# Causal mask of a differential-attention kernel: a TensorE matmul into the score block in place of a VectorE add

## The chip, the cores and the metric

One core of one Trainium2 chip runs the whole step as one program. The metric is the device time of that program in microseconds (us). TensorE (PE) multiplies, VectorE (DVE), ScalarE (ACT) and GpSimd (POOL) do the rest, SyncE (SP) issues most transfers. Each engine works through its own instructions in order and waits on semaphores for the others. A matmul has a weight operand, loaded into TensorE first (LDWEIGHTS, shown as PEld), and a moving operand that is streamed through it; products are summed in PSUM.

## The reference, cut to what matters

One inference step of a two-layer trunk with D = 1024 and a prompt of 1024 tokens: a matrix-memory layer, then a differential-attention layer, plus eight decode sequences. The change touches only the attention of the prompt. For each of 8 heads there are two sets of queries and keys (c = 0 and 1, 64 columns each), a causal softmax over each, and a difference of the two weights:

```python
def diff_mix(q, k_parts, v_parts, masks, lam):
    scores = []
    for kp, mk in zip(k_parts, masks):
        s = jnp.einsum('bqhcd,bkhcd->bhcqk', q, kp).astype(F32) * ATTN_SCALE
        if mk is not None:
            s = jnp.where(mk, s, -jnp.inf)        # mask = qpos >= kpos
        scores.append(s)
    p = jax.nn.softmax(jnp.concatenate(scores, axis=-1), axis=-1)
    w = p[:, :, 0] - lam * p[:, :, 1]
...
        o = jnp.einsum('bhqk,bkhe->bqhe', w[..., start:start + s_len].astype(vp.dtype), vp)
```

All is held to float32; the kernel splits operands into a high part and a remainder (names ending in H and L), so a product becomes three matmuls: high by high, high by low, low by high.

## The kernel before, in words

The phases follow each other: norm, gates, matrix memory for the prompt, the same for the samples, its output projection, then `attention_phase` (the one touched), decode, and the last projection.

`attention_phase` goes head by head. Head 0's `sweep1` comes first; then a hardware loop (`Fori` in `heads`) runs `sweep2(h)` and `sweep1(h+1)` for h = 0 to 6; head 7's `sweep2` and a `tail` follow as straight code. The order on each engine is simply the order of the code; semaphores tie the engines together.

- `sweep1` projects queries and keys (`project(0, t)`: 24 matmuls of 256 columns for each of nine token blocks), rotates them on VectorE and transposes them into `QTH`, `QTL`, `KTH`, `KTL`. There the two components lie on partitions 0 to 63 (c = 0) and 64 to 127 (c = 1).
- `sweep2` takes the eight query blocks t = 0 to 7 in turn. On TensorE the order for t is `scores(h, t)` (L1836), `turn_weights(h, t-1)` (transposes, L1857), `project_values(t+1)` (24 matmuls, L1831), `turn_output(h, t-2)` (L1877), `weigh(h, t-1)` (weights by values, L1869).
- `scores` computes for each c the block's scores against all keys up to the diagonal: three matmuls with 64 weight rows (L1846) for each chunk of up to 512 columns. The width is rounded up to a multiple of 256: 256 columns at t = 0 and 1, 512 at 2 and 3, 768 (a chunk of 512 and one of 256) at 4 and 5, 1024 at 6 and 7. The two components write different PSUM tensors, `S[0]` and `S[1]`. The last matmul of each component raises `sc`.
- VectorE, on `sc`, adds the triangular mask `cst[:, C_MB:...]` (0 or -1e30) to the diagonal 128 columns of `S[c]` in PSUM (L1792), takes the row maximum (L1794) and scales it (L1795, raises `mxs`). `links.link` makes the next instruction wait until the linked one has ended.
- ScalarE exponentiates on `mxs` (L1634) and raises `ex`. VectorE then cuts the next head's weights (L1696), forms the difference of the two softmaxes (L1809 to L1812, raises `ww`), and `turn_weights` on TensorE waits for `ww`.
- `scores(h, t)` itself waits for `ex` of block t-1, since it overwrites `S[c]`; `project_values(t+1)` waits for `vz`, the evacuation of the values by ScalarE (L1584 to L1586).

Of the kernel before, what the change touches and what calls it, by code (L numbers as in the profile page):

```python
# [17 lines left out]
ALU = mybir.AluOpType  # L18
ACT = mybir.ActivationFunctionType
F32 = mybir.dt.float32  # L20
F32R = mybir.dt.float32r
# [3 lines left out]
P = 128  # L25
# [21 lines left out]
C_MB = C_MA + P  # L47
# [59 lines left out]
def trunk_step(  # L107
# [8 lines left out]
    def sb(name, shape, dt=F32):  # L116
        return ctx.enter_context(nc.sbuf_tensor(name, shape, dt))
# [3 lines left out]
    def sem(name):  # L121

        held.append(nc.alloc_semaphore(name=name))
        return held[-1]
# [3 lines left out]
    def phase_tensor(name, shape, dt=F32):  # L128

        return scratch[-1].enter_context(nc.sbuf_tensor(name, shape, dt))  # L130
# [13 lines left out]
    def two(name):  # L144
        return [sem(f"{name}{k}") for k in range(2)]
# [12 lines left out]
    with ctx:  # L158

        cst = sb("cst", [P, C_N])  # L160
        ident = cst[:, C_ID:C_ID + P]
# [1316 lines left out]
        def attention_phase():  # L1478
# [14 lines left out]
            KR = RAW[:, 4 * KT * P:5 * KT * P].rearrange("p (t c) -> p t c", t=NT)  # L1493
            QTR = phase_tensor("QTR", [P, 2, SEQ], F32R)
            QTH, QTL = QTR[:, 0, :], QTR[:, 1, :]
            KTH = WH[:, 4 * KT * P:5 * KT * P]
            KTL = WL[:, 4 * KT * P:5 * KT * P]
            N = 2 * P
# [4 lines left out]
            pj, rope, kr, kth, vz, sc, mxs, ex, ww, av, ot, otf, sq, rr, sg, gz, yy, smd = (  # L1503
                sem(f"c_{s}") for s in ("pj", "rope", "kr", "kth", "vz", "sc", "mx", "ex", "w", "av",
                                        "ot", "otf", "sq", "rr", "sg", "gz", "y", "sm"))
            tr, trf, wt, wte = two("c_tr"), two("c_trf"), two("c_wt"), two("c_wte")
            dch, pch = sem("c_dve"), sem("c_pool")
            B_V, B_O = BK[0], BK[1]
            S = [PD[c][:, :, :].rearrange("p a n -> p (a n)") for c in range(2)]
# [3 lines left out]
            def heads(eng, sweep1, sweep2, tail, links=None, per=0):  # L1513

                sweep1(0, None)
                with eng.Fori(0, H - 1) as h:
                    if links:
                        links.enter(h, per)
                    sweep2(h, False)
                    sweep1(h + 1, h)  # L1520
                if links:
                    links.leave(H - 1)
                sweep2(H - 1, True)
                tail(H - 1)

            with nc.Block() as block:
# [40 lines left out]
                def _(act):  # L1567
                    def cut(r, k):
                        for j, (_, _, g) in enumerate(PARTS[r]):
                            cols = slice(j * P, (j + 1) * P)  # L1570
                            act.activation(reg(WH, r)[:, k, cols], reg(RAW, r)[:, k, cols], ACT.Copy,
                                           scale=g[:, k:k + 1]).then_inc(hi[r], 1)

                    act.wait_ge(lamS, 1)
                    act.activation(le, mx, ACT.Exp).then_inc(lamE, 1)

# [26 lines left out]
                    def sweep1(h, before):  # L1603
                        act.wait_ge(c_w[1], 32 * (h + 1))
                        act.wait_ge(pj, 2 * NB * h)
                        for t in range(NB):
# [6 lines left out]
                            if t >= 1:  # L1613
                                c = t - 1
                                act.wait_ge(tr[c % 2], 4 * h + c // 2 + 1)
                                act.activation(QTH[:, c * P:(c + 1) * P], BK[2 + c % 2][:, 0:P], ACT.Copy)
                                act.activation(KTH[:, c * P:(c + 1) * P], BK[2 + c % 2][:, P:2 * P], ACT.Copy)\
                                   .then_inc(kth, 1)
# [68 lines left out]
                def _(dve):  # L1687
                    v = nc.vector
                    links = Chain(dve, dch)
# [58 lines left out]
                    def weights(h, c):  # L1748

                        m = c - 3  # L1750
                        dve.wait_ge(wt[1], 4 * h + m)
                        v.tensor_copy(WT[:, 4:4 + m, :], BK[3][:, 0:m * P].rearrange("p (a c) -> p a c", a=m))\
                         .then_inc(wte[1], 1)

                    def sweep1(h, before):
                        for t in range(NB):
# [11 lines left out]
                            if t >= 1:  # L1768
# [3 lines left out]
                                v.tensor_tensor(QTL[:, tt], BK[2 + c % 2][:, 0:P], QTH[:, tt].bitcast(F32), ALU.subtract)  # L1772
                                v.tensor_tensor(KTL[:, tt], BK[2 + c % 2][:, P:2 * P], KTH[:, tt].bitcast(F32),
                                                ALU.subtract).then_inc(trf[c % 2], 1)
# [7 lines left out]
                    def sweep2(h, last):  # L1782
                        for t in range(NB):
                            n = (t + 1) * P
                            if t < NT:
                                for c in range(2):
                                    if c == 1 and t > 4:
                                        weights(h, t - 1)
                                    if c == 1 and t >= 2:
                                        output(h, t - 2)  # L1790
                                    dve.wait_ge(sc, 2 * (NT * h + t) + c + 1)
                                    links.link(v.tensor_tensor(S[c][:, n - P:n], S[c][:, n - P:n],  # L1792
                                                               cst[:, C_MB:C_MB + P], ALU.add))
                                    links.link(v.tensor_reduce(mx[:, c:c + 1], S[c][:, 0:n], AX, ALU.max, negate=True))  # L1794
                                    v.tensor_scalar(nm[:, c:c + 1], mx[:, c:c + 1], ATTN_SCALE, None, ALU.mult)\  # L1795
                                     .then_inc(mxs, 1)
                            if t == NT:
                                output(h, t - 2)
                            if t >= 3:
                                o_transposed(h, t - 3)  # L1800
                            if t >= 1:
                                sigmoid(h, t - 1)
                            if t < NT:
                                if not last:
                                    cut(0, t, h)

                                b = t % 2
                                dve.wait_ge(ex, 2 * (NT * h + t) + 2)
                                links.link(v.reciprocal(cf, sm[:, 1:2]))  # L1809
                                links.link(v.scalar_tensor_tensor(cf, sm[:, 0:1], nl, cf, ALU.mult, ALU.mult))  # L1810
                                v.reciprocal(rc[:, b:b + 1], sm[:, 0:1])
                                v.scalar_tensor_tensor(PR[:, 0, 0:n], PR[:, 1, 0:n], cf, PR[:, 0, 0:n],  # L1812
                                                       ALU.mult, ALU.add).then_inc(ww, 1)
                                dve.wait_ge(ww, NT * h + t + 1)

                    def tail(h):
# [1 line left out]
                        output(h, NT - 1)  # L1818
                        o_transposed(h, NT - 2)
                        o_transposed(h, NT - 1)  # L1820
                    heads(dve, sweep1, sweep2, tail, links, 9 + 8 * 2 * 2 + 16)

                @block.tensor
                def _(pe):
# [11 lines left out]
                    def scores(h, t):  # L1836
                        width = (t // 2 + 1) * 2 * P
                        for c in range(2):

                            pe.wait_ge(ex, 2 * NT * h + max(2 * t - 1 + c, 0))  # L1840
                            rows = slice(DK * c, DK * c + DK)
                            for at in range(0, width, 512):
                                kk = slice(at, min(at + 512, width))
                                i = 0
                                for q, k in ((QTH, KTH), (QTH, KTL), (QTL, KTH)):
                                    x = nc.tensor.matmul(S[c][:, kk], q[rows, t * P:(t + 1) * P], k[rows, kk],  # L1846
                                                         start=(i == 0), stop=(i == 2))
                                    i += 1
                            x.then_inc(sc, 1)

                    def turn_weights(h, c):
                        pe.wait_ge(ww, NT * h + c + 1)
# [51 lines left out]
                    def sweep2(h, last):  # L1904
                        def project_values(t):

                            pe.wait_ge(vz, NT * h + t)
                            pe.wait_ge(smd, h)
                            project(1, t, B_V)

                        pe.wait_ge(hi[1], 2 * KT * (h + 1))
                        pe.wait_ge(lo[1], 2 * KT * (h + 1))
                        project_values(0)
                        for b in range(2):
                            pe.wait_ge(trf[b], 4 * (h + 1))
                        pe.wait_ge(rope, NB * (h + 1))
                        scores(h, 0)
                        project_values(1)
                        for t in range(1, NT):
                            scores(h, t)  # L1920
                            turn_weights(h, t - 1)
                            project_values(t + 1)
                            if t >= 2:
                                turn_output(h, t - 2)
                            weigh(h, t - 1)
# [400 lines left out]
        run(out_phase, "oa", w_out_a, True)  # L2326
        fresh_semaphores()
        run(attention_phase)
        run(decode_phase)
        run(out_phase, "ob", w_out_b, False)  # L2330
# [31 lines left out]
```

## Time and profile before

| | |
|---|---|
| median of 3 runs | 2084.65 us (2083.03 to 2088.9) |
| span of the profiled execution, first to last instruction | 2078.4 us |
| PE busy over the span | 1826.7 us, 88% |
| DVE busy | 1153.2 us, 55% |
| ACT busy | 806.3 us, 39% |
| mean granted TensorE clock | 0.928 |

The page gives the profiled execution's span and no separate run time for it; the median lies 6.25 us above the span, which is what lies around it. The attention of the prompt runs from about 950 us to 1643 us of the span; its `sweep2` work begins at 986 us. Busy time of a matmul group is the union of its records, and records of pipelined matmuls overlap; for what a matmul costs in a stream, the distance between two starts is to be read, not the duration.

### The profile page before, as it was taken

How to read it: one execution, taken by the hardware profiler on the slowest of the kernel's cores; microseconds unless marked ns; L12 is line 12 of the kernel's file. 1: busy time of each engine (PE TensorE's matmuls, PEld its weight loads, DVE VectorE, ACT ScalarE, POOL GpSimd, SP SyncE). 2: the span in 40 equal slices, each digit the busy share in tenths (PEclk: the TensorE clock that was granted, in tenths of full speed). 3: DMA queues.
4: the chain of work that ended last, by engine and by line, in shares of the span. 5: the costliest groups of instructions: out<-in, count | busy, mean ns of one | idle time of the engine just before them, and what ended most of it. 6: DMA issues, size and time to landing. Idle time of an engine off the chain costs nothing. (4 is left out here: it accounts for less than half of the span.)

```text
span 2078.4 us, 40295 instructions
## 1 busy us (share of the span) xinstructions
PE 1826.7 (88%) x13011; PEld 1669.8 (80%) x13011; DVE 1153.2 (55%) x3279; ACT 806.3 (39%) x2208; POOL 379.9 (18%) x823
## 2 busy tenths in 40 slices
PE   5499999999999675998999999999999688888598
PEld 4399999999999564998889898898989666665398
DVE  4443544443443354246767667676677566666533
ACT  5333333333333223033534435344353356666401
POOL 1021221221221121011312213122131100101101
PEclk8699999999999776999999999999999888989699
DMA  4213113113211134222011120111200267777522
GB/s 118 64 32 65 31 33 65 34 30 65 34 30 15 39 88 131 78 103 87 26 50 32 31 63 12 51 32 31 63 12 11 82 228 257 257 243 241 157 73 84
DMA packets 157012, 165.21 MB, mean 79 GB/s; under 512 B 12314, under 2 KB 134266, under 8 KB 156914
## 3 DMA queue, kind: packets, MB, share of 16 engines
q1 hardware_dynamic: 152610, 159.85, 26.2%
q0 software_dynamic: 1184, 4.23, 0.8%
q8 instruction: 39, 0.64, 0.1%
q14 instruction: 59, 0.48, 0.1%
q10 hardware_dynamic: 3120, 0.01, 0.1%
HBM read 138.69 MB, written 25.37 MB: 79 GB/s over the span
## 5 line engine op out<-in xcount | busy, mean ns | idle before, releaser
L809 PE MATMUL PS<-WH,XH 128*128 128x384 f32 (+3 forms) x1152 | 369.4, 321 | 1.8 <-DVE WORK L731 1.8
L809 PE MATMUL PS<-WL,XH 128*128 128x384 f32 (+3 forms) x1152 | 356.9, 310 | 0.0
L809 PE MATMUL PS<-WH,XL 128*128 128x384 f32 (+3 forms) x1152 | 356.6, 310 | 0.0
L809 PEld LDWEIGHTS PS<-WH,XH 128*128 128x128 f32 (+1 forms) x1152 | 208.1, 181 | 6.6 <-DVE WORK L731 2.2
L809 PEld LDWEIGHTS PS<-WL,XH 128*128 128x128 f32 (+1 forms) x1152 | 208.2, 181 | 4.1
L809 PEld LDWEIGHTS PS<-WH,XL 128*128 128x128 f32 (+1 forms) x1152 | 207.8, 180 | 4.6
L1432 PE MATMUL PS<-WH,XH 128*128 128x256 f32 (+1 forms) x576 | 166.2, 289 | 34.4 <-DVE WL L1305 28.6
L1831 PE MATMUL PS<-WH,XH 128*128 128x256 f32 (+1 forms) x576 | 173.6, 301 | 2.3 <-ACT WORK L1586 2.1
L1831 PE MATMUL PD<-WH,XH 128*128 128x256 f32 (+1 forms) x576 | 169.4, 294 | 2.9 <-PEq L142 2.9
L1831 PE MATMUL PS<-WL,XH 128*128 128x256 f32 (+1 forms) x576 | 167.4, 291 | 0.0
L1831 PE MATMUL PS<-WH,XL 128*128 128x256 f32 (+1 forms) x576 | 167.0, 290 | 0.0
L1432 PE MATMUL PS<-WL,XH 128*128 128x256 f32 (+1 forms) x576 | 165.3, 287 | 0.0
L1432 PE MATMUL PS<-WH,XL 128*128 128x256 f32 (+1 forms) x576 | 164.0, 285 | 0.0
L1831 PE MATMUL PD<-WL,XH 128*128 128x256 f32 (+1 forms) x576 | 163.9, 284 | 0.0
L1831 PE MATMUL PD<-WH,XL 128*128 128x256 f32 (+1 forms) x576 | 163.6, 284 | 0.0
L1432 PEld LDWEIGHTS PS<-WH,XH 128*128 128x128 f32 (+1 forms) x576 | 106.3, 185 | 37.9 <-issue 33.0
L1634 ACT ACTIVATE WORK<-PD,WORK 128x256 f32<-128x256 f32 (+7 forms) x128 | 95.0, 742 | 82.0 <-DVE WORK L1795 81.3
L2258 PE MATMUL PS<-cst,RAW 128*128 128x128 f32 x512 | 87.3, 322 | 40.3 <-DVE XL L2165 35.9
L2258 PEld LDWEIGHTS PS<-cst,RAW 128*128 128x128 f32 x512 | 68.4, 164 | 58.5 <-DVE XL L2165 42.8
L1831 PEld LDWEIGHTS PS<-WH,XH 128*128 128x128 f32 (+1 forms) x576 | 108.8, 189 | 4.8 <-ACT WORK L1586 3.9
L1831 PEld LDWEIGHTS PS<-WH,XL 128*128 128x128 f32 (+1 forms) x576 | 108.9, 189 | 0.7
L1831 PEld LDWEIGHTS PS<-WL,XH 128*128 128x128 f32 (+1 forms) x576 | 108.8, 189 | 0.6
(335 smaller groups left out, 4411.3 us busy)
## 6 DMA issues: line engine op xcount, KB each, us to landing
RAW<-in_cache_k SPq DMA_DIRECT2D x64, 512.0 KB, 4.5
WORK<-in_cache_v SPq DMA_DIRECT2D x64, 512.0 KB, 4.4
RAW<-in_w_in_a SPq DMA_DIRECT2D x40, 512.0 KB, 6.3
RAW<-in_w_in_b SPq DMA_DIRECT2D x16, 512.0 KB, 6.3
RAW<-in_w_kv SPq DMA_DIRECT2D x16, 512.0 KB, 5.2
out<-WORK SPq DMA_DIRECT2D x16, 512.0 KB, 2.9
WORK<-in_x_prompt SPq DMA_DIRECT2D x8, 512.0 KB, 4.9
WORK<-d_G SPq DMA_DIRECT2D x8, 512.0 KB
```

The costliest lines, as they stand in the source:

```text
L809: last = nc.tensor.matmul(bank[0:rows, 0:n], x[:, k, tt], reg(w)[:, k, :], start=(i == 0), stop=(i == 3 * KT - 1))
L1432: last = nc.tensor.matmul(BK[u % 2][0:rows, 0:N], x[:, k, tt], reg(w, r)[:, k, :], start=(n == 0), stop=(n == 3 * KT - 1))
L1634: act.activation(PR[:, c, 0:(t + 1) * P], S[c][:, 0:(t + 1) * P], ACT.Exp, scale=ATTN_SCALE, bias=nm[:, c:c + 1], accum_out=sm[:, c:c + 1] ...
L1831: last = nc.tensor.matmul(bank[0:rows, 0:N], x[:, k, tt], reg(w, r)[:, k, :], start=(i == 0), stop=(i == 3 * KT - 1))
L2258: x = nc.tensor.transpose(BK[j][:, h * P:(h + 1) * P], KB[:, p % 4, (4 * j + h) * P:(4 * j + h + 1) * P], ident)
```

## The change

ScalarE copies the identity and the mask once, at the start of the phase, into a new tensor `MR` of TensorE's input type. After the score matmuls of a component, TensorE multiplies the identity (128 weight rows by 128 columns) with the mask (128 columns) and lets the product accumulate onto the diagonal columns of `S[c]`; that matmul now raises `sc`. VectorE's add is gone. The number of linked instructions that VectorE counts per loop turn falls by 16.

```diff
+            MR = phase_tensor("MR", [P, 2, P], F32R)
...
+            mr = sem("c_mr")
...
+                    act.activation(MR[:, 0, :], ident, ACT.Copy)
+                    act.activation(MR[:, 1, :], cst[:, C_MB:C_MB + P], ACT.Copy).then_inc(mr, 1)
                     act.wait_ge(lamS, 1)
...
                                     dve.wait_ge(sc, 2 * (NT * h + t) + c + 1)
-                                    links.link(v.tensor_tensor(S[c][:, n - P:n], S[c][:, n - P:n],
-                                                               cst[:, C_MB:C_MB + P], ALU.add))
                                     links.link(v.tensor_reduce(mx[:, c:c + 1], S[c][:, 0:n], AX, ALU.max, negate=True))
...
-                    heads(dve, sweep1, sweep2, tail, links, 9 + 8 * 2 * 2 + 16)
+                    heads(dve, sweep1, sweep2, tail, links, 9 + 8 * 2 + 16)
...
-                                    x = nc.tensor.matmul(S[c][:, kk], q[rows, t * P:(t + 1) * P], k[rows, kk],
-                                                         start=(i == 0), stop=(i == 2))
+                                    nc.tensor.matmul(S[c][:, kk], q[rows, t * P:(t + 1) * P], k[rows, kk],
+                                                     start=(i == 0), stop=(i == 2))
                                     i += 1
-                            x.then_inc(sc, 1)
+                            nc.tensor.matmul(S[c][:, t * P:(t + 1) * P], MR[:, 0, :], MR[:, 1, :], start=False, stop=True,
+                                             skip_group_check=True).then_inc(sc, 1)
...
+                        pe.wait_ge(mr, 1)
                         scores(h, 0)
```

On TensorE, at `scores(h, 2)` inside the loop, the program before has the three matmuls of c = 0, those of c = 1 and then the transposes (the rows name output and operands; L1840 sets a register for a wait):

```order
L1846 MATMUL PD<-WH,QTR 128x512
L1846 MATMUL PD<-WL,QTR 128x512
L1846 MATMUL PD<-WH,QTR 128x512
L1840 REGISTER_ALU
L1846 MATMUL PD<-WH,QTR 128x512
L1846 MATMUL PD<-WL,QTR 128x512
L1846 MATMUL PD<-WH,QTR 128x512
L1857 MATMUL PS<-cst,WORK 128x128 x2
```

The same place in the changed program, where lines below the edits count a few higher:

```order
L1848 MATMUL PD<-WH,QTR 128x512
L1848 MATMUL PD<-WL,QTR 128x512
L1848 MATMUL PD<-WH,QTR 128x512
L1851 MATMUL PD<-MR 128x128
L1842 REGISTER_ALU
L1848 MATMUL PD<-WH,QTR 128x512
L1848 MATMUL PD<-WL,QTR 128x512
L1848 MATMUL PD<-WH,QTR 128x512
L1851 MATMUL PD<-MR 128x128
L1860 MATMUL PS<-cst,WORK 128x128 x2
```

One matmul of 128 weight rows now stands between the two components, and one between the second component and the transposes.

On VectorE, at the start of a query block in the loop before:

```order
L1792 TENSOR_TENSOR PD<-PD,cst 128x128
L97 REGISTER_ALU
L1794 TENSOR_REDUCE WORK<-PD 128x1
L97 REGISTER_ALU
L1795 TENSOR_SCALAR WORK<-WORK 128x1
```

and in the changed program:

```order
L1796 TENSOR_REDUCE WORK<-PD 128x1
L97 REGISTER_ALU
L1797 TENSOR_SCALAR WORK<-WORK 128x1
```

The add and the wait for its end are gone from the head of the chain; nothing else on VectorE has moved.

## Rows read from the trace of the kernel before

**Rows 1.** The page: its head line.

```profile
span 2078.4 us, 40295 instructions
```

**Rows 2.** Busy time by engine in one window: time, busy time (instructions), clock, DMA.

```profile
985.00:1640.00 655.00, 625.00 (x4842) 578.67 (x4841) 463.09 (x1513) 292.31 (x983) 154.83 (x373) 0.98 0.13 35
```

**Rows 3.** DVE groups, 985 to 1640 us: count, busy us, mean ns, idle before.

```profile
L1792 DVE TENSOR_TENSOR PD<-PD,cst 128x128 f32<-128x128 f32 x128 | 37.9, 296 | 61.6 <-issue 33.4 <-PE PD L1846 24.4
```

**Rows 4.** PE waits, 985 to 1640 us: total us, times, longest.

```profile
PE PD L1846 <- ACT WORK L1634: 11.5, 6, 2.2
...
PE PS L1877 <- DVE YX L1738: 2.7, 9, 0.7
```

**Rows 5.** PE in order of time, scores(3, 2): start, us, instruction.

```profile
1255.21 0.50 PE L1846 MATMUL PD<-WH,QTR 64*128 64x512 f32 x2
1255.55 0.40 PE L1846 MATMUL PD<-WL,QTR 64*128 64x512 f32 x2
1255.78 0.40 PE L1846 MATMUL PD<-WH,QTR 64*128 64x512 f32 x2
1256.11 0.44 PE L1857 MATMUL PS<-cst,WORK 128*128 128x128 f32 x2
```

**Rows 6.** PE in order of time, a stream of projection matmuls before transposes.

```profile
1297.49 0.28 PE L1831 MATMUL PD<-WH,XL 128*128 128x256 f32 x1
1297.61 1.03 PE L1857 MATMUL PS<-cst,WORK 128*128 128x128 f32 x8
1298.40 0.36 PE L1831 MATMUL PD<-WH,XH 128*128 128x256 f32 x1
```

**Rows 7.** PE in order of time, weights by values (eight products, sixteen records).

```profile
1301.44 1.95 PE L1869 MATMUL PS<-WORK 128*128 128x128 f32 x16
1303.23 0.27 PE L1901 MATMUL PS<-cst,WORK 128*128 128x128 f32 x1
```

**Rows 8.** PE in order of time, scores(3, 3).

```profile
1259.94 0.51 PE L1846 MATMUL PD<-WH,QTR 64*128 64x512 f32 x2
...
1261.32 0.55 PE L1857 MATMUL PS<-cst,WORK 128*128 128x128 f32 x3 [0.41 <-DVE WORK L1812]
```

**Rows 9.** PE in order of time, scores(3, 4).

```profile
1265.46 0.49 PE L1846 MATMUL PD<-WH,QTR 64*128 64x512 f32 x1
...
1267.08 0.28 PE L1846 MATMUL PD<-WH,QTR 64*128 64x256 f32 x1
1267.29 0.66 PE L1857 MATMUL PS<-cst,WORK 128*128 128x128 f32 x4
```

**Rows 10.** PE in order of time, scores(3, 7).

```profile
1286.49 0.50 PE L1846 MATMUL PD<-WH,QTR 64*128 64x512 f32 x1
...
1288.66 0.98 PE L1857 MATMUL PS<-cst,WORK 128*128 128x128 f32 x7
```

**Rows 11.** All engines in order of time, head 3 from block 0 to 1.

```profile
1246.20 0.30 DVE L1792 TENSOR_TENSOR PD<-PD,cst 128x128 f32<-128x128 f32 x1 [5.22 <-issue]
1246.53 0.29 DVE L1794 TENSOR_REDUCE WORK<-PD 128x1 f32<-128x128 f32 x1
...
1247.55 0.39 PE L1846 MATMUL PD<-WH,QTR 64*128 64x256 f32 x1 [1.58 <-ACT WORK L1634]
...
1250.26 0.33 PE L1857 MATMUL PS<-cst,WORK 128*128 128x128 f32 x1 [1.33 <-DVE WORK L1812]
```

**Rows 12.** PE in order of time, head 7, blocks 0 and 1.

```profile
1587.97 0.39 PE L1846 MATMUL PD<-WH,QTR 64*128 64x256 f32 x2
1588.19 0.29 PE L1846 MATMUL PD<-WL,QTR 64*128 64x256 f32 x2
1588.31 0.28 PE L1846 MATMUL PD<-WH,QTR 64*128 64x256 f32 x2
1588.74 0.39 PE L1831 MATMUL PS<-WH,XH 128*128 128x256 f32 x1
```

**Rows 13.** PE in order of time, the tail of head 7.

```profile
1635.09 1.09 PE L1857 MATMUL PS<-cst,WORK 128*128 128x128 f32 x8 [0.75 <-DVE WORK L1812]
```

## The prediction

> **What bounds the kernel now.** I began with the head line of the page for the span [rows 1], then took the busy time of the stretch from 985 to 1640 us, in which the score blocks lie. TensorE is busy for 625 of 655 us there and VectorE for 463, at a mean granted clock of 0.98, so nearly all of it at the 2.4 GHz level [rows 2]. TensorE is the bound of the stretch: what the change puts on it counts, and what it takes from VectorE counts only where TensorE stood waiting for VectorE. Next I took VectorE's group of mask adds, to see what is removed: 128 adds, 37.9 us busy, and VectorE idle 61.6 us before them [rows 3]. An engine that sits idle in front of the instruction is not short of time for it. Then TensorE's waits: those before the scores sum to 11.5 us in six times, and those before the output transposes to 2.7 us in nine [rows 4]. Last, TensorE in order of time through single score blocks, since the cost lies in how these matmuls follow each other.
>
> That view shows what decides the case. For block 2 the six score matmuls of 512 columns start in pairs: two at 1255.21, two at 1255.55, two at 1255.78, and the transposes follow at 1256.11 [rows 5]. By the program, three of them are of c = 0 and the other three, behind these, of c = 1. The two components have 64 weight rows each, on different halves of the array, and run side by side: six matmuls take 0.90 us, where the spacing of one component alone is 0.34, 0.23 and 0.33. From the same rows, a component of one 512 chunk takes 0.90 us whether or not the other runs beside it; so the second component is free. The new mask matmul has 128 weight rows, stands between the two components in program order, and needs both halves.
>
> The rule of the Trainium skill that speaks to this is in "TensorEngine Tiling (Array Packing)", section Tiling Modes: tiles work independently of each other, and a change of tiling mode drains the engine. The pairs agree with its first half [rows 5], and so do the 0.34 us after the first matmul of a mode against 0.23 later with its second.
>
> **The change part by part.** (1) *The overlap goes.* After the change the order is c = 0, mask, c = 1, mask, transposes. The first mask must wait for all of c = 0, and c = 1 waits behind it. Call B the time of one component, from its first start to the start of a 128-row matmul behind it. For blocks 2 and 3, B = 0.90 [rows 5]. For blocks 4 and 5 three matmuls of 256 columns are added at 0.12 us, the spacing of such matmuls in a stream [rows 6]: 1.26. For 6 and 7 three more of 512 at 0.23 [rows 5]: 1.59. For blocks 0 and 1 (256 columns) 0.22 + 0.12 [rows 12] plus the 0.21 from a last 256-column matmul to the transposes [rows 9]: 0.55. Return to 64 rows after the first mask costs 0.09 more than a start behind a matmul of the same mode; I take it from the exit, 0.33 against 0.23 [rows 5] or 0.21 against 0.12 [rows 9, 6].
>
> (2) *The mask matmul itself*, m. No matmul of this operand type with only 128 moving columns is in the trace. From below: a transpose with the same shape, one record each, 0.79 us for eight or 0.10 us, say 0.11 [rows 6]. From above: a float32 product of that shape, two records each, 1.79 us for eight or 0.22 us [rows 7]. Nothing excludes either. The code itself rounds score widths up to 256 columns, which pays only if narrower matmuls of this type gain nothing; and a 256-column one takes 0.12. I take 0.22, the row that is a matmul and not a transpose.
>
> So a score block costs 2B + 2m + 0.09 = 2B + 0.53 where nothing hides it:
> - block 2: 1.80 + 0.53 = 2.33, before 0.90 [rows 5]: +1.43
> - block 3: 2.33, before 1.38, of which 0.41 was a wait for VectorE that the longer block now covers [rows 8]: +0.95
> - blocks 4 and 5: 2.52 + 0.53 = 3.05, before 1.83 [rows 9]: +1.22 each
> - blocks 6 and 7: 3.18 + 0.53 = 3.71, before 2.17 [rows 10]: +1.54 each
>
> Together 7.90 us a head. Blocks 0 and 1 of heads 1 to 6 cost nothing: at each turn of the loop VectorE starts some 5 us late (5.22 idle on nothing that the profile shows, at 1246.20), and TensorE then stands 1.58 us before the scores of block 1 and 1.33 us before the transposes of block 0 [rows 11]. Six such stalls are what stands in the waits before the scores [rows 4]. Block 0 grows by about 0.9 us, block 1 by at most 1.1, and both fall into these waits.
>
> (3) *What VectorE gives back.* An add and its link take 0.33 us, from 1246.20 to 1246.53 [rows 11]. Where TensorE waits on this chain the gain is two adds, 0.65 us, once a loop head, at the transposes of block 0. Elsewhere TensorE doesn't wait for the chain, and it is worth nothing. The short waits before the output transposes, 2.7 us in nine [rows 4], are covered by the longer block 7: 0.23 a head, which leaves part of the tail's.
>
> A loop head then costs 7.90 - 0.65 - 0.23 = 7.02 us; six of them 42.1 us. Heads 0 and 7 have no late start. Head 7's block 0 took 0.77 with its wait [rows 12] and now 2 x 0.55 + 0.53 = 1.63: +0.86; block 1 about +1.1 (0.55 before, by B, without the wait); block 3 had no wait there, +1.43; so 0.86 + 1.1 + 1.43 + 1.43 + 5.52 = 10.3. In its tail TensorE waited 0.75 us for VectorE's last weights [rows 13]; VectorE now ends 0.2 to 0.65 us earlier, and with the 0.23 about 1.0 comes back: 9.3. Head 0 has the two small waits of blocks 2 and 3 instead; I take 9.3 for it too.
>
> Sum: 42.1 + 18.6 = 60.7 us. With m = 0.11, 104 exposed masks (12 in each loop head, 16 in each of the other two) cost 11.4 us less: 49. If no wait covers anything, the six loop heads pay 0.65 + 0.23 + 0.43 and up to 2 us more each, some 80 in all; I see no reason for that but keep it as the far end.
>
> (4) *Edits at nothing.* ScalarE's two copies into `MR` stand at the start of the phase, before it waits for the transfers of the lambda vectors, and TensorE's wait on them ends long before the first scores. If that cover were gone they cost well under 1 us, once. The new operand of the mask matmul needs no transfer. The semaphore now comes 0.3 to 0.5 us later for c = 0 and later still for c = 1; behind it on VectorE are the maximum, the output scaling and the next head's weight cuts, but without the adds VectorE reaches the weights at about the same time, and TensorE asks for them 1 to 1.5 us later.
>
> The span goes from 2078.4 to 2139 us [rows 1]; the median stands 6.25 us above the span, so 2145 us.
>
> **The rivals.** *The second component passes the mask* (the halves stay side by side because TensorE orders the work by array half and the mask costs its own place only). Then a block costs 2m more: 12 masks a head at 0.11 to 0.22 is 1.3 to 2.6 us, less about 1.3 a loop head for the waits; in all +3 to +15 us, 2088 to 2100. For it: TensorE already starts c = 1 ahead of two earlier matmuls of c = 0 [rows 5]. Against it: the mask reads and fills both halves, so c = 1's weights would overwrite it. The skill's page "TensorE: Matmul & The Clock Gate", Part 3, has matmuls start strictly in program order; by that rule there would be little overlap to lose and this rival's time would come out. The pairs that start together do not agree with it [rows 5].
>
> *VectorE's chain is what TensorE waits for* and the masks hide in the remaining waits. That ends faster: 0.65 and 0.23 for six loop heads, 0.41 at block 3 in seven heads and the tail's 0.75 give about -9 us, 2076. It decides if the masks run within the waits of blocks 0, 1 and 3. For it: those waits exist [rows 8, 11]. Against it: blocks 2 and 4 to 7 have none [rows 5, 9, 10].
>
> *Every change of mode costs more than the rows show*, because two full changes now stand in each block with weights of both kinds. At 0.2 us more for each of the 104 exposed masks, twice the 0.1 that a change of mode shows [rows 5], this is +21 us on the forecast, 2166.
>
> **How the numbers follow.** Forecast 0.80, with its own range 2130 to 2160 (m from 0.11 to 0.22 and more of the waits used up or left); second component passes 0.12, a third of it within 0.3%; VectorE's chain 0.04, three quarters of it beyond 0.3%; dearer changes of mode 0.04. A change of 0.3%, 6 us, is about what a measurement of this kernel can tell from none. Faster 0.03, same 0.05, slower 0.92. The range 2115 to 2165 holds most of the forecast and the dear case and stops short of the cheap ones.
>
> **What would show it.** Right: in the changed profile the scores of c = 1 start after the first mask of the block; block 2 takes 2.2 to 2.4 us from first score to transposes, block 6 about 3.6; the waits before the transposes of block 3 are gone; VectorE's idle time before the maximum grows. Wrong: score matmuls still in pairs; a stretch from 985 us that is not longer by 45 to 65 us; a mask matmul that follows the last score at a distance beyond 0.4 us; or a gain before the transposes of block 0 in place of a loss.

## The result, and the profile after

The changed kernel takes 2121.8 us (median of 4 runs, 2115.55 to 2128.17) against 2084.09 us for the kernel before (4 runs): a ratio of 1.0172, 95% interval 1.0152 to 1.0192. It is slower by some 37 us (38 by the medians, 36 by the ratio). The forecast was 2145 us, slower by 61; the direction and the mechanism came out, the size was too large by 23. The measured time lies within the stated range of 2115 to 2165, but below the 2130 to 2160 that the forecast gave for itself.

The head line of its page, then its busy time by engine in the window of the score blocks (time, busy us and instructions of PE, PEld, DVE, ACT and POOL, granted clock, DMA):

```profile
span 2119.2 us, 40320 instructions
```

```profile
993.00:1683.00 690.00, 676.23 (x4960) 612.99 (x4959) 426.30 (x1384) 284.59 (x984) 142.23 (x376) 1.00 0.12 33
```

TensorE is now busy for 676 of 690 us where it was for 625 of 655 [rows 2]; VectorE has lost 37 us of work, and the stretch has become longer all the same. Two details matter below: TensorE's idle time fell from 30 to 14 us, and the mean granted clock rose from 0.98 to 1.00.

VectorE's maximum, now the first of its chain, by count, busy us, mean ns and idle before it with its releasers:

```profile
L1796 DVE TENSOR_REDUCE WORK<-PD 128x1 f32<-128x256 f32 (+7 forms) x128 | 96.7, 755 | 98.6 <-PE PD L1851 63.1 <-issue 33.6
```

VectorE waits 63.1 us for the mask matmul (L1851) where it waited 24.4 us for the scores, then in front of its add [rows 3]. The work taken from it turned into waiting.

TensorE in order of time through block 2 of head 3 (start, duration, instruction), the place of [rows 5]:

```profile
1273.05 0.50 PE L1848 MATMUL PD<-WH,QTR 64*128 64x512 f32 x1
1273.39 0.39 PE L1848 MATMUL PD<-WL,QTR 64*128 64x512 f32 x1
1273.62 0.39 PE L1848 MATMUL PD<-WH,QTR 64*128 64x512 f32 x1
1273.94 0.33 PE L1851 MATMUL PD<-MR 128*128 128x128 f32 x1
1274.20 0.49 PE L1848 MATMUL PD<-WH,QTR 64*128 64x512 f32 x1
1274.53 0.39 PE L1848 MATMUL PD<-WL,QTR 64*128 64x512 f32 x1
1274.77 0.39 PE L1848 MATMUL PD<-WH,QTR 64*128 64x512 f32 x1
1275.09 0.33 PE L1851 MATMUL PD<-MR 128*128 128x128 f32 x1
1275.25 0.40 PE L1860 MATMUL PS<-cst,WORK 128*128 128x128 f32 x2
```

No pair starts together any more. Component 0 takes 0.89 us to its mask, component 1 starts 0.26 us behind that mask and takes 0.89 us to the second one: 2.20 us to the transposes instead of 0.90. Block 7 of the same head, the place of [rows 10], goes from 2.17 to 3.62 us:

```profile
1309.00 0.50 PE L1848 MATMUL PD<-WH,QTR 64*128 64x512 f32 x1
...
1312.62 0.51 PE L1860 MATMUL PS<-cst,WORK 128*128 128x128 f32 x3
```

The start of that head, the place of [rows 11]:

```profile
1266.41 0.29 DVE L1796 TENSOR_REDUCE WORK<-PD 128x1 f32<-128x128 f32 x1 [5.45 <-issue]
...
1267.44 0.39 PE L1848 MATMUL PD<-WH,QTR 64*128 64x256 f32 x1 [0.96 <-ACT WORK L1638]
...
1269.61 0.33 PE L1860 MATMUL PS<-cst,WORK 128*128 128x128 f32 x1 [0.49 <-DVE WORK L1814]
```

VectorE still starts late. From its first instruction to the transposes it is 3.20 us, before 4.06: the shorter chain shows here. TensorE's own waits in the whole stretch, engine and line, what for, total us, times, longest:

```profile
PE PD L1848 <- ACT WORK L1638: 6.8, 6, 1.5
PE PS L1860 <- DVE WORK L1814: 3.7, 7, 0.7
PE PS L1880 <- DVE YX L1742: 0.7, 1, 0.7
```

They answer to 11.5 us before the scores and 2.7 us before the output transposes [rows 4], and to this line of the same view before, for the waits ahead of the transposes of the weights:

```profile
PE PS L1857 <- DVE WORK L1812: 11.1, 14, 1.3
```

From the first scores of head 0 to the last output transpose it is 690.8 us (992.94 to 1683.73) against 656.1 (986.22 to 1642.29): +34.7 us. The spans differ by 40.8 us: 6.7 us more stand before the first scores, and 0.6 us less behind the last output transpose. The change has only ScalarE's two copies into `MR` there, which end at 956.1 us, some 37 us ahead of the first scores; over the profiles of this study the first scores start between 983.0 and 993.3 us, at 991.3 in one without those copies (filled waits, below). The 6.25 us that were said to lie around the span are not all of that kind: in the runs whose time and span are both known the two are 1.7 us apart (2120.93 and 2119.2 us for the profiled run here). By the same distance the execution profiled before would have taken 2080.1 us (an estimate), 4.5 us below its median, so the difference of the two spans is larger than that of the times.

### The profile page after: what moved, and what is told of

It is laid out like the page before. It is cut to its first block and busy times, and to the rows that moved or that the text cites. A ratio compares the mean times of both kernels' runs of the same rounds, so it can differ in the third digit from the quotient of the medians.

```text
span 2119.2 us, 40320 instructions
## 1 busy us (share of the span) xinstructions
PE 1883.3 (89%) x13139; PEld 1709.0 (81%) x13139; DVE 1115.8 (53%) x3151; ACT 799.0 (38%) x2210; POOL 366.2 (17%) x823
## 5 line engine op out<-in xcount | busy, mean ns | idle before, releaser
L809 PEld LDWEIGHTS PS<-WH,XH 128*128 128x128 f32 (+1 forms) x1152 | 208.0, 181 | 7.3 <-DVE WORK L731 2.9
L809 PEld LDWEIGHTS PS<-WL,XH 128*128 128x128 f32 (+1 forms) x1152 | 208.2, 181 | 4.1
L809 PEld LDWEIGHTS PS<-WH,XL 128*128 128x128 f32 (+1 forms) x1152 | 207.5, 180 | 4.6
L1432 PE MATMUL PS<-WH,XH 128*128 128x256 f32 (+1 forms) x576 | 166.3, 289 | 34.9 <-DVE WL L1305 28.8
L1833 PE MATMUL PS<-WH,XH 128*128 128x256 f32 (+1 forms) x576 | 168.7, 293 | 0.0
L1796 DVE TENSOR_REDUCE WORK<-PD 128x1 f32<-128x256 f32 (+7 forms) x128 | 96.7, 755 | 98.6 <-PE PD L1851 63.1
L1848 PE MATMUL PD<-WH,QTR 64*128 64x512 f32 (+1 forms) x384 | 136.4, 389 | 6.8 <-ACT WORK L1638 6.8
L1432 PEld LDWEIGHTS PS<-WH,XH 128*128 128x128 f32 (+1 forms) x576 | 106.4, 185 | 38.3 <-issue 33.1
L1833 PEld LDWEIGHTS PD<-WH,XH 128*128 128x128 f32 (+1 forms) x576 | 105.3, 183 | 3.4 <-issue 3.0
```

What stands on the lines that cost most here:

```text
L809: last = nc.tensor.matmul(bank[0:rows, 0:n], x[:, k, tt], reg(w)[:, k, :], start=(i == 0), stop=(i == 3 * KT - 1))
L1432: last = nc.tensor.matmul(BK[u % 2][0:rows, 0:N], x[:, k, tt], reg(w, r)[:, k, :], start=(n == 0), stop=(n == 3 * KT - 1))
L1833: last = nc.tensor.matmul(bank[0:rows, 0:N], x[:, k, tt], reg(w, r)[:, k, :], start=(i == 0), stop=(i == 3 * KT - 1))
```

## The experiments

Three questions were open: whether the cost is the cut overlap or the mask matmul itself; what VectorE's relief was worth; and why the loss was 35 us where the sum had said 61.

**Masks behind both components.** Both mask matmuls of a block stand behind the scores of both components; nothing else differs from the changed kernel.

```diff
+                        for c in range(2):
                             nc.tensor.matmul(S[c][:, t * P:(t + 1) * P], MR[:, 0, :], MR[:, 1, :], start=False, stop=True,
                                              skip_group_check=True).then_inc(sc, 1)
```

> The two mask matmuls stand behind the scores of both components (c = 0, c = 1, mask 0, mask 1). Theory (the loss is the overlap of the two 64-row components, cut by a 128-row matmul between them): score matmuls start in pairs again; block 2 takes 0.90 + 0.22 = 1.12 us from first score to transposes instead of 2.20, block 7 about 2.4 instead of 3.62; the whole is 2074 to 2090 us, the loss of 37 us all but gone. Rival (the mask matmul itself is what costs, 0.27 us or more for each of 104): pairs may come back, but the time stays at 2105 to 2118.

2079.14 us, ratio to before 0.9978 (0.9965 to 0.9991). TensorE in order of time, block 2 of head 3:

```profile
1256.13 0.50 PE L1848 MATMUL PD<-WH,QTR 64*128 64x512 f32 x2
1256.46 0.40 PE L1848 MATMUL PD<-WL,QTR 64*128 64x512 f32 x2
1256.69 0.40 PE L1848 MATMUL PD<-WH,QTR 64*128 64x512 f32 x2
1257.03 0.44 PE L1852 MATMUL PD<-MR 128*128 128x128 f32 x2
1257.30 0.41 PE L1861 MATMUL PS<-cst,WORK 128*128 128x128 f32 x2
```

The pairs are back, the two masks cost 0.27 us, and the whole loss of 37 us has gone with one change of order. The same 128 mask matmuls run in both kernels, so the overlap is what the change paid with. The new order also saves changes between 64 and 128 weight rows, but these are the smaller part: of the 1.03 us between 2.20 and 1.17 us for block 2, 0.89 is the time of component 1, and 0.15 is what the two masks take more between the components than side by side (0.26 + 0.16 us from each mask to the next start, against 0.27 for both).

**Each mask twice.** The changed kernel with a second, equal mask matmul behind each; the masked scores get -2e30.

> The changed kernel with each mask matmul issued twice (the masked scores get -2e30). It measures one mask in a stream: 104 exposed. At 0.11 us each (the pace of a transpose) 11 us above the changed kernel, 2133; at the 0.22 that the prediction took, 23 us, 2145.

2131.32 us, ratio 1.0232 (1.0212 to 1.0252), about 0.6% or 12 us above the changed kernel's ratio. TensorE, block 2 of head 3, from the first mask on:

```profile
1280.25 0.33 PE L1851 MATMUL PD<-MR 128*128 128x128 f32 x1
1280.42 0.28 PE L1853 MATMUL PD<-MR 128*128 128x128 f32 x1
1280.62 0.50 PE L1848 MATMUL PD<-WH,QTR 64*128 64x512 f32 x1
```

The start of component 1 moves from 0.26 us behind the first mask to 0.37: a mask in a stream is 0.11 us, the lower bound of the prediction, not the 0.22 that it took. The starts decide this rather than the whole time, since in this profile all six loop heads also lose time to the clock (below), which only two do in the changed kernel's.

**No mask at all.** The kernel before without VectorE's add and with nothing in its place (the attention is not causal within the diagonal block).

```diff
-                                    links.link(v.tensor_tensor(S[c][:, n - P:n], S[c][:, n - P:n],
-                                                               cst[:, C_MB:C_MB + P], ALU.add))
```

> The kernel before with VectorE's add left out and nothing in its place, so the attention of the prompt is not causal within the diagonal block. It shows what the removal alone gives. Theory (VectorE is off the path but for the start of each loop head, and the waits there also lower TensorE's clock for 3.4 to 6.8 us each): 9 us from the waits and some of the 12 us that the six half-clock stretches cost, 2064 to 2075. Rival without the clock: the waits alone, 2073 to 2077. Rival that VectorE's chain is the bound: 38 us or more, below 2046.

2060.12 us, ratio 0.9899 (0.9879 to 0.9919), below the 2064 to 2075 expected. The relief of VectorE is worth 21 us, more than the waits alone (9) that the prediction's rival had counted and less than the adds' 38 us. The half-clock stretches, places behind the start of heads 1 to 6 where the granted clock is at the 1.2 GHz level (shown under the filled waits), had no part in it; all six were still there. Reading the starts of each block from the trace in order of time, a loop head (one of heads 1 to 6, from its first scores to those of the next head) loses 2.8 us: 0.9 at its start, 0.5 before the transposes of block 2, and 1.4 us in the late blocks 5 to 7, where the prediction had counted 0.23.

**The kept add.** The changed kernel with VectorE's add as well, to see what covers those late waits.

> The changed kernel with VectorE's add kept as well (the mask is applied twice, the masked scores get -2e30). It asks what covers the short waits of blocks 5 to 7 in the changed kernel. If it is the longer score blocks, the stretches from the transposes of blocks 4, 5 and 6 stay at 4.74, 5.08 and 8.37 us, and only the start of a loop head gets 0.6 us longer, six times: 2124 to 2130 with the clock as it falls. If it is the shorter VectorE chain, they go back to 5.2, 5.5 and 8.9 and the whole to 2133 to 2138.

2138.41 us, ratio 1.0242 (1.0226 to 1.0258). Neither expectation holds alone. From the transposes of block 4, 5 and 6 to the next block (the last to the transposes of block 7), means of heads 1 to 6: before 5.22, 5.54 and 8.94 us; changed 4.74, 5.08 and 8.37; with the add kept 4.74, 5.33 and 8.70. The longer score blocks cover 0.93 of the 1.51 us, and with them in place the shorter VectorE chain gives the other 0.58. These are not two separate shares: without a mask, with short score blocks, the shorter chain alone took 1.40 us off the same stretches (4.79, 5.10 and 8.41), and with the masks behind both components it took 0.64 (4.81, 5.43 and 8.82).

**The early copy** (e5 in the later expectations). The kernel before, with VectorE's copy of the transposed output ahead of the maximum of c = 1.

```diff
                                     if c == 1 and t >= 2:
                                         output(h, t - 2)
+                                    if c == 1 and t >= 3:
+                                        o_transposed(h, t - 3)
...
-                            if t >= 3:
+                            if t == NT:
                                 o_transposed(h, t - 3)
```

> The kernel before with one move in VectorE's order: the copy of the transposed output (o_transposed of block t-3) stands ahead of the maximum of c = 1 instead of behind it. Theory (in blocks 5 to 7 TensorE waits shortly for that copy because VectorE's chain, mask adds included, holds it up; the removed adds repaid this too, about 1.4 us a head): the stretches from the transposes of block 4, 5 and 6 to the next block fall from 5.22, 5.54 and 8.94 to about 4.8, 5.1 and 8.4 us, the whole by 8 to 12 us, to 2071 to 2076. Rival (those stretches are TensorE's own work): no change, 2083.

2084.77 us, ratio 1.0010 (0.9998 to 1.0022): no gain. The first two stretches fell as expected, to 4.78 and 5.11, so TensorE had waited there for this copy. But the third rose, from 8.94 to 9.68 us, and the copy now stands ahead of the maximum. TensorE, block 7 of head 3, in order of time:

```profile
1291.45 0.50 PE L1848 MATMUL PD<-WH,QTR 64*128 64x512 f32 x1
...
1294.11 0.66 PE L1859 MATMUL PS<-cst,WORK 128*128 128x128 f32 x4 [0.42 <-DVE WORK L1814]
```

Block 7 takes 2.66 us where it took 2.17 [rows 10], and a loop head 87.55 us where it took 86.79. TensorE now waits 0.42 us for VectorE before the transposes there. The wait only moved.

**Filled waits** (e4). The kernel before, with 10 matmuls of 256 columns before the scores of block 1 and 8 before the transposes of block 0, into columns of `S[0]` that nothing reads.

```diff
+                    def warm(n):
+                        for _ in range(n):
+                            nc.tensor.matmul(S[0][:, 512:512 + N], XH[:, 0, 0:P], reg(WH, 1)[:, 0, :], start=True, stop=True)
...
+                            if t == 1:
+                                warm(10)
                             scores(h, t)
+                            if t == 1:
+                                warm(8)
                             turn_weights(h, t - 1)
```

> The kernel before with idle TensorE time filled: 10 matmuls of 256 columns into unused columns of S[0] before the scores of block 1 and 8 before the transposes of block 0, in every head; their results are overwritten unread. Theory (the 2.9 us of waits at a loop head are followed by a half-clock stretch, and this is what the changed kernel got rid of): the six stretches between 1070 and 1520 us go or shrink to a few, loop heads 1.5 to 2.5 us shorter, heads 0 and 7 up to 2 us longer each; 2070 to 2080. Rival (the clock has no part in it): 2084 to 2090, since the added matmuls can only cost.

2077.37 us, ratio 0.9967 (0.9953 to 0.9982): a kernel with more work is faster. The reason is in the stretch from the transposes of block 0 to the scores of block 2, which holds the same instructions in every head. The kernel before, in heads 1 to 3 (columns as above, the granted clock third from the end):

```profile
1076.04:1081.35 5.31, 5.31 (x27) 5.19 (x27) 3.38 (x13) 1.99 (x7) 0.92 (x2) 0.58 0.01 2
1163.08:1169.09 6.01, 6.01 (x27) 5.79 (x27) 3.38 (x13) 1.99 (x7) 0.92 (x2) 0.50 0.00 1
1250.26:1255.21 4.95, 4.95 (x27) 4.80 (x27) 3.37 (x13) 1.99 (x7) 0.92 (x2) 0.66 0.01 2
```

The same with filled waits, heads 1 to 3:

```profile
1083.07:1087.64 4.57, 4.57 (x29) 4.45 (x28) 3.38 (x13) 1.99 (x7) 0.92 (x2) 0.70 0.01 2
1168.97:1172.41 3.44, 3.44 (x27) 3.29 (x27) 2.43 (x9) 1.99 (x7) 0.92 (x2) 1.00 0.01 2
1253.81:1257.25 3.44, 3.44 (x28) 3.29 (x28) 2.44 (x9) 1.99 (x7) 0.92 (x2) 1.00 0.01 2
```

All six heads of the loop lose time there before, two of six here. Behind the waits at the head's start, in which TensorE had stood still for 1.6 to 2.2 and again 0.9 to 1.3 us, the granted clock drops to the 1.2 GHz level for part of the stretch or all of it, and 3.44 us become 4.8 to 6.0. Heads 0 and 7, which have no such waits, take 3.44 and 3.49 us.

**The changed kernel once more,** with no edit.

> The changed kernel once more, for its clock record. If the fall from six to two half-clock stretches at the loop heads belongs to the change, one to three stretches again; if it was chance, up to six, and the time goes up with them by some 1.6 us for each 3.4 us at half clock, 2122 to 2129.

2120.98 us, one run. The changed kernel's first profile in heads 1 to 3:

```profile
1088.90:1092.35 3.45, 3.45 (x27) 3.30 (x28) 2.43 (x11) 1.99 (x7) 0.92 (x2) 1.00 0.01 2
1178.63:1183.59 4.96, 4.96 (x28) 4.81 (x28) 2.78 (x11) 1.99 (x7) 0.92 (x2) 0.66 0.01 2
1269.61:1273.05 3.44, 3.44 (x27) 3.29 (x28) 2.40 (x11) 1.99 (x7) 0.92 (x2) 1.00 0.01 2
```

Two of its six heads are at the lower clock there, three in this second profile (4.94, 4.98 and 4.95 us). With each mask twice and with the add kept, all six are, though in the first of these TensorE stands still for less: 0.7 to 1.1 and then 0.26 us at the start of a head, against 0.7 to 1.5 and 0.49 in the changed kernel. Within the changed kernel's first profile, head 1 stood longest (1.53 us) and kept its clock, and head 5 stood shortest (0.71) and lost it. Without a mask, with the masks behind both components and in the hybrid below the waits are on the mean shorter than before as well, and all six heads still fall. So how long TensorE stood does not by itself tell whether the clock drops; that stays open, and with it how much of the changed kernel's gain here is its own and how much is chance.

**Mask matmul for blocks 0 and 1 only** (e6, the hybrid; both masks behind both components), VectorE's add for the rest. The edit is shown against the kernel before; `MR` and the wait on it are as in the change.

```diff
+                                    if t >= 2:
                                         links.link(v.tensor_tensor(S[c][:, n - P:n], S[c][:, n - P:n],
...
-                            x.then_inc(sc, 1)
+                            if t >= 2:
+                                x.then_inc(sc, 1)
+                        for c in range(2 if t < 2 else 0):
+                            nc.tensor.matmul(S[c][:, t * P:(t + 1) * P], MR[:, 0, :], MR[:, 1, :], start=False, stop=True,
+                                             skip_group_check=True).then_inc(sc, 1)
```

> Mask matmul only for blocks 0 and 1 of a head (both masks behind both components), VectorE's add for the rest. Theory: at the start of a loop head the shorter chain gives 0.6 to 0.8 us in six heads, the matmuls hide there; heads 0 and 7 pay 0.3 to 0.5 us each; with half-clock stretches as before 2078 to 2081, down to 2072 if some of the stretches go. Rival (a mask matmul costs wherever it stands): 2085 to 2090.

2077.42 us, ratio 0.9968 (0.9957 to 0.9979). From the first scores of a loop head to the transposes of block 0 it is 7.90 us against 8.68, within the 0.6 to 0.8 us forecast. Heads 0 and 7 lose 0.1 us or less each where 0.3 to 0.5 had been expected.

**The three together** (e7). The edit above, the early copy, and shorter filled waits:

```diff
+                                    if c == 1 and t >= 3:
+                                        o_transposed(h, t - 3)
...
+                            if t == 1 and not last:
+                                warm(8)
                             scores(h, t)
+                            if t == 1 and not last:
+                                warm(5)
                             turn_weights(h, t - 1)
```

> The hybrid of e6 with the early copy of e5 and filled waits at the loop heads (8 matmuls before the scores of block 1, 5 before the transposes of block 0, not in the last head). If the three gains are separate they add: 4 + 10 + 8 us off, 2058 to 2066, below every kernel but the one without a mask. If they share a wait, 2068 to 2075.

2074.86 us, ratio 0.9959 (0.9946 to 0.9971). They did not add: the early copy brings its new wait along here too (block 7 at 2.79 us). So the copy goes back to its old place:

```diff
-                                    if c == 1 and t >= 3:
-                                        o_transposed(h, t - 3)
...
-                            if t == NT:
+                            if t >= 3:
                                 o_transposed(h, t - 3)
```

> The hybrid with filled waits of e7, without the early copy. The early copy cost 0.76 us a head net in e5, so a loop head of 84.1 us where e7 has 84.87, and 5 us less in all: 2068 to 2072. If the early copy cost nothing beside the hybrid: 2075 as e7.

2074.39 us beside 2088.13 for the kernel before in those runs, ratio 0.9931 (0.9917 to 0.9944): the fastest complete kernel of the study, 0.7% under the kernel before and 2.4% under the changed one by the ratios. Its loop head takes 84.42 us against 86.79, with one of six at the lower clock; with the early copy it was 84.87, so that copy cost 0.45 us a head here where 0.76 had been expected. Its stretch of the score blocks:

```profile
990.00:1640.00 650.00, 632.98 (x4984) 586.92 (x4982) 455.78 (x1491) 292.48 (x986) 155.54 (x376) 0.99 0.13 36
```

## Why the prediction was right in kind and too high in size

The mechanism came out as put: the pairs are gone, c = 1 starts behind the first mask, the block times of 2.20 and 3.62 us lie where "2.2 to 2.4" and "about 3.6" had them, the wait at block 3 is covered, VectorE idles in front of its maximum. The rival in which the second component passes the mask fell with the first block of the trace. The Trainium skill's page "TensorEngine Tiling (Array Packing)", section Tiling Modes, lets a change of tiling mode drain the engine; the trace agrees (0.26 us from the mask to a 64-row matmul, 0.17 from a mask to a second mask where it stands twice). The Trainium skill's page "TensorE: Matmul & The Clock Gate", Part 3, lets matmuls start strictly in program order, by which there was little overlap to lose; the some 40 us between the two orders of the masks do not agree with it.

Two of the four signs that the prediction had named for being wrong came as well. The stretch is longer by 34.7 us and not by 45 to 65, which says that the size was off. And there is a gain of 0.81 us before the transposes of block 0; its own sum had forecast 0.65 there, so this sign contradicted the sum and tells nothing against the mechanism. That the time lies within 2115 to 2165 is in part luck: the range went down to 2115, though no case worked out in the prediction gave a time between 2100 and 2130, and even the sum with the cheaper mask, 49 us, gives some 2134.

The sum, by its own steps (us; a loop head stands six times; measured as the difference of the two profiles from starts in order of time, means of heads 1 to 6):

| step | predicted | measured |
|---|---|---|
| blocks 2 to 7, first score to transposes | +7.90 | +7.20 |
| first scores to the transposes of block 0 | -0.65 | -0.81 |
| transposes of block 0 to the scores of block 2 | 0 | -1.39 |
| all other stretches up to the transposes of block 7 | -0.23 | -1.66 |
| one loop head | +7.02 | +3.34 |
| head 0 | +9.3 | +6.7 |
| head 7 with the tail | +9.3 | +8.0 |
| all heads | +60.7 | +35 |

1. *The mask's price.* 0.11 us in a stream, shown by the doubled mask; 0.22 was the wrong end. The row that it came from has sixteen records for eight products [rows 7], so 0.11 us for each record, and a mask leaves one record. The remark that columns under 256 gain nothing spoke for the 0.12 us of a 256-column matmul, and not for 0.22. By the prediction's own count of 104 this is 11 us; against it stands some 0.06 us that a 128-row matmul pays behind 64-row ones (0.17 instead of 0.11), which I had left out. In the blocks the error is 0.70 us a head, 4 us in six, and some more in heads 0 and 7.

2. *The late waits.* The step "2.7 us in nine, 0.23 a head" failed. It took TensorE's waits from the matmul's list alone. The wait before the output transposes also stands in the list of weight loads, without a releaser. Before (weight loads, 985 to 1640 us):

```profile
PEld PS L1877 <- issue: 5.7, 18, 0.6
PEld PS L1869 <- issue: 4.8, 22, 0.7
```

After, the first of them is gone and of the second this is left:

```profile
PEld PS L1872 <- issue: 2.1, 8, 0.7
```

Single rows show such a wait without any note of it, before in block 5 of head 3: the transpose starts 0.26 us behind the last projection matmul and the next matmul 0.33 us behind the transpose, where 0.11 to 0.12 is the pace.

```profile
1276.91 0.27 PE L1831 MATMUL PS<-WH,XL 128*128 128x256 f32 x1
1277.17 0.30 PE L1877 MATMUL PS<-cst,WORK 128*128 128x128 f32 x1
1277.50 0.35 PE L1869 MATMUL PS<-WORK 128*128 128x128 f32 x1
```

The three late stretches give 1.51 us a loop head and all of that row of the table 1.66, where 0.23 had been counted: 1.43 a head, some 9 us in six. That the wait is for VectorE's copy of the transposed output is shown by the early copy; it is covered from two sides, by the longer blocks and by the shorter chain.

3. *The clock.* The prediction read 0.98 as "nearly all at 2.4 GHz" and went on. The missing 2% sat in one place, behind the stalls that the change shortens: 1.39 us a loop head, 8 us in six (1.14 us a head in the second profile of the changed kernel). That filling these waits alone raises the clock is shown by the filled kernel; that the changed kernel would always keep it is not, nor that shorter stalls are what kept it.

With 1 us from the row before the transposes of block 0 (0.16 a head) these make 4 + 9 + 8 + 1 = 22 us for the loop heads; the other 4 of the 26 are in heads 0 and 7. For head 0 the price of head 7 had been taken, but head 0 has the late waits of the loop heads and got 1.46 us back in them.

## What to carry to other kernels

Before a matmul goes between two groups that use different halves of the array, look at the starts: if they pair from the first on, as in block 2, the second group is free, and one full-height matmul between them buys its own 0.1 us at the price of the second group's whole time (0.89 us). Work moved off an engine with slack is worth only the places where the full one waits for it; find these in single rows by the distance between starts, for here the list of TensorE's own waits showed 2.7 us of some 10. A mean clock of 0.98 over a long stretch can be one short place at half clock in every turn of a loop.

## What the runs showed of the hardware that was not expected

- Two groups of 64-row matmuls on different halves start together although one stands three matmuls behind the other in the program; six of 512 columns take 0.90 us, the same as three. With six in each group the second starts together with the third matmul of the first, 0.57 us behind its start (block 7 before; its first row is in [rows 10]):

```profile
1287.06 0.63 PE L1846 MATMUL PD<-WH,QTR 64*128 64x512 f32 x3
```

- A matmul with 128 moving columns of this operand type costs 0.11 us in a stream, about as much as a one-pass transpose of that shape (0.10 to 0.11) and a little less than a 256-column one (0.12).
- Behind stalls of 1.6 to 2.2 and 0.9 to 1.3 us the granted clock dropped to half in all six turns of the loop, at a cost of 1.4 to 2.6 us each, and 18 idle matmuls in these stalls (13 in the fastest kernel) brought that down to two turns, and one.
